# The product of P and V moved ahead of the next item's scores in the slots of the mixing stage

## The reference, cut to what matters

```python
# first model: heads of 64, each query sees a window of keys, with a learned bias
s = jnp.einsum('bhrqd,bhrwkd->bhrqwk', qb, kb).astype(jnp.float32) * scale
s = s + bias[None].astype(jnp.float32)
p = jax.nn.softmax(s.reshape(B, H, rows, COL_BLOCK, wh * COL_SLAB), axis=-1)
outs.append(jnp.einsum('bhrqwk,bhrwkd->bhrqd', p, vb))
# second model: 4 heads of forgetting attention, 4 of dilated attention with rotated q and k
p = jax.nn.softmax(jnp.where(mask, s, NEG_BIG), axis=-1)
return jnp.einsum('bhqk,bhkd->bhqd', p.astype(v.dtype), v)
```

## Time and profile before

| | us |
|---|---|
| median of 3 runs | 2108.96 |
| lowest, highest | 2106.34, 2109.08 |
| the profiled execution | 2110.61 |
| its span, first to last instruction | 2108.8 |
| TensorE busy with matmuls | 2048.7 (97%) |
| VectorE busy | 1310.0 (62%) |
| ScalarE busy | 1058.2 (50%) |
| mean granted clock of TensorE | 0.988 of 2.4 GHz |

### The profile page before, as it was taken

One profiled execution on the slowest core, in us unless ns is written; L12 is line 12 of the kernel. 1 busy time (PEld: TensorE's weight loads), 2 busy tenths in 40 slices (PEclk: granted clock), 3 DMA queues, 4 the chain that ended last, 5 costly groups with the idle time before them and its releaser, 6 DMA issues.

```text
span 2108.8 us, 26738 instructions
## 1 busy us (share of the span) xinstructions
PE 2048.7 (97%) x11144; PEld 1714.2 (81%) x11144; DVE 1310.0 (62%) x1532; ACT 1058.2 (50%) x1278; POOL 56.6 (3%) x72
## 2 busy tenths in 40 slices
PE   7999999999999999999999999999999999999998
PEld 5888877888888887788788888878888889887886
DVE  5655866555655686655565568765556556976554
ACT  4444565444544556544454456654454445565443
POOL 3200004000000000000000000000000000000000
PEclk9999999999999999999999999999999999999999
DMA  8654336555555433555455543345545554335551
GB/s 279 214 195 162 140 112 178 185 187 192 179 181 194 156 131 110 183 181 195 164 177 182 193 156 136 116 169 191 183 176 198 182 184 175 121 121 182 188 181 59
DMA packets 52217, 357.81 MB, mean 170 GB/s; under 512 B 6592, under 2 KB 7008, under 8 KB 9600
## 3 DMA queue, kind: packets, MB, share of 16 engines
q1 hardware_dynamic: 48960, 350.25, 46.6%
q0 software_dynamic: 2416, 5.51, 1.3%
q10 hardware_dynamic: 720, 0.34, 0.1%
HBM read 355.02 MB, written 1.05 MB: 169 GB/s over the span
## 4 chain that ended last, share of the span: by engine, by line
PE 88%; DVE 6%; ACT 3%; DVEq 1%; issue 1%; DMA 0%; ACTq 0%
PE bank L360 82%; DVE w_lo L1087 2%; PE bank L464 2%; PE bank L520 1%; PE bank L404 1%; ACT w_hi L747 1%; PE bank L601 1%; DVE h_lo L1104 1%; PE bank L566 1%; DMA cos_sin<-positions 0%; PE bank L587 0%; ACT h_hi L767 0%; DVEq L1275 0%; ACTq L920 0%; ACT arena L935 0%
## 5 line engine op out<-in xcount | busy, mean ns | idle before, releaser
L1087 DVE TENSOR_TENSOR w_lo<-raw,w_hi 128x2048 fp32r<-128x2048 f32 x332 | 762.7, 2297 | 387.8 <-ACT w_hi L747 387.4
L747 ACT ACTIVATE w_hi<-raw 128x2048 fp32r<-128x2048 f32 x332 | 634.3, 1911 | 270.9 <-PE bank L360 260.7
L360 PE MATMUL bank<-w_hi,h_hi 128*128 128x512 f32 x1536 | 611.7, 398 | 7.1 <-DVE w_lo L1087 4.1
L360 PE MATMUL bank<-w_hi,h_lo 128*128 128x512 f32 x1536 | 600.4, 391 | 0.0
L360 PE MATMUL bank<-w_lo,h_hi 128*128 128x512 f32 x1536 | 599.7, 390 | 0.0
L360 PEld LDWEIGHTS bank<-w_hi,h_hi 128*128 128x128 f32 x1536 | 289.4, 188 | 71.0 <-DVE w_lo L1087 10.2
L360 PEld LDWEIGHTS bank<-w_hi,h_lo 128*128 128x128 f32 x1536 | 289.0, 188 | 62.1
L360 PE MATMUL bank<-w_hi,act_hi 128*128 128x512 f32 x832 | 330.4, 397 | 6.3 <-DVE act_lo L1384 6.3
L360 PEld LDWEIGHTS bank<-w_lo,h_hi 128*128 128x128 f32 x1536 | 289.8, 189 | 56.5
L360 PE MATMUL bank<-w_lo,act_hi 128*128 128x512 f32 x832 | 326.1, 392 | 0.0
L360 PE MATMUL bank<-w_hi,act_lo 128*128 128x512 f32 x832 | 326.1, 392 | 0.0
(11 more groups left out here) (195 smaller groups left out, 1460.7 us busy)
## 6 DMA issues: line engine op xcount, KB each, us to landing
raw<-stream SPq DMA_DIRECT2D x332, 1024.0 KB, 4.8
arena<-rpb POOLq DMA_DIRECT2D x32, 96.0 KB, 9.3
x<-xt SPq DMA_DIRECT2D x4, 256.0 KB, 7.0
arena<-final_gain POOLq DMA_DIRECT2D x2, 512.0 KB, 4.5
out<-x SPq DMA_DIRECT2D x4, 256.0 KB, 2.8
arena<-c_level POOLq DMA_DIRECT2D x1, 384.0 KB, 3.4
arena<-code_w POOLq DMA_DIRECT2D x2, 128.0 KB, 3.6
arena<-c_att POOLq DMA_DIRECT2D x1, 256.0 KB, 5.0
```

The costliest lines, as they stand in the source:

```text
L360: last = mm(o, a, r, start=start and n == 0, stop=stop and n == len(pairs) - 1)
L747: fn(w_hi[u % SLOTS][:, :], raw[u % RAW][:, :], ACT.Copy).then_inc(hi_done, 1)
L1087: tt(w_lo[u % SLOTS][:, :], raw[u % RAW][:, :], w_hi[u % SLOTS][:, :].bitcast(F32), ALU.subtract).then_inc(lo_done, 1)
```

## The change

In `slot`, the call of `heads` for the item that was transposed at the slot's beginning is moved from behind `scores` (and behind the rotation in slot 9) to a place ahead of both. The transposes and the recurrence's step stay in front of it. No instruction is added or removed, and the lists of the other engines are the same.

```diff
                 if i in SPAN_AFTER[b]:
                     span_step(b, L, SPAN_AFTER[b][i])
+                if turned is not None:
+                    heads(b, L, turned)
                 if item is not None:
                     scores(b, L, item)
                 if b == 1 and i == ROTATE_AFTER:
...
-                if turned is not None:
-                    heads(b, L, turned)
                 if i == RECURRENCE_AFTER[b]:
                     recurrence_out(b, L)
```

## The result

| | before | after |
|---|---|---|
| median (20 runs each) | 2107.30 | 2111.49 |
| lowest, highest | 2103.37, 2112.57 | 2110.04, 2114.07 |
| the profiled execution, its span | 2110.61, 2108.8 | 2110.04, 2108.3 |
| mean granted clock | 0.988 | 0.991 |

The changed kernel is slower by a ratio of 1.0020, with a 95% interval of 1.0013 to 1.0027: 4.2 us, between 2.7 and 5.7. Equal times lie outside the interval; the size is the 0.2% that the prediction took as the least to be told from it. A single pair of executions of this kernel can't be compared by its end, since the runs of one kernel spread over 9 us (before) and 4 us (after).

A forecast was written before the change was run, and what follows sets the result against it. TensorE's own work was taken to bound the kernel (88% of the last-ending chain). Stalls of 1.9 for the first model's two layers plus 2.2 and 2.1 for the second's gave +6.2 us, from 2108.96 to 2115.2; range 2109.5 to 2120.5.

The forecast's parts named there:

- slot 11 of the second model: Largest single term, 0.87: copy ends later because the heads delay the rotation by 0.37, and scores no longer fill the wait.
- Slots 5 to 9 of the first model: Heads wait for the copy that scores had covered: 0.27 in slot 5, 0.13 in 6 to 8, 0.27 in 9.
- slots 14 and 15 of the second: Slot 14: heads already wait for the copy, scores now follow them, 0.55 lost; slot 15: unchanged.
- slot 11 of the first: Scores move into TensorE's 2.55 wait for the mixed result, which ends when it did: 0.
- rival D: Late scores delay the next copy in some 9 more slots by 0.4: +3.6 on top, 2118.8; chance 0.05.
- of the exchanged pieces themselves nothing is gained or lost: Every slot: scores (0.63) and heads (0.59) both still run, so swapping them costs only the stall for the copy.
- Slot 13 of the second model: Copy's end plus 0.05 falls after the scores' old start, so TensorE stalls 0.15.
- Slot 10 of the first model: Long recurrence step covers the copy, and TensorE waits 0.36 for VectorE's copy L1247 anyway: 0.
- rival C: Stalls smaller or partly absorbed, as other engines reach later waits with the delay already paid: +3.1, 2112.1; chance 0.12.
- slot 7 of the second model: Heads stall for the copy after losing the scores as cover: 0.61 in the first layer, 0.54 in the second.
- Rival A: Splitting the first model's slot 11 pause avoids low clock: 2109.6 (both layers) or 2112.4 (one); chance 0.18.
- Rival B: Second model's slot 11 pause grows to about 1.5 and the clock falls: +9 to +11.8, 2118 to 2120.8; chance 0.10.

The follow-up runs named there:

- spare matmuls: Both orders with unread matmuls added in TensorE's pauses: 2098.38 with the old order (ratio 0.9961 to the kernel before), 2104.17 with the new order (0.9988).
- The run with the new order in the covered slots: Old order with unread matmuls in TensorE's pauses, heads moved ahead only in slots 10 (first model), 8 and 12 (second): 2097.71 against 2098.38 without the move.
- the second model alone: Kernel before, with heads moved ahead of the scores in the second model's slots only: 2111.31 against 2107.64, ratio 1.0020.
- the first model alone: Kernel before, with heads moved ahead of the scores in the first model's slots only: 2108.58 against 2107.64, ratio 1.0002.

## Why the prediction held, point by point

**Direction and mechanism: right.** The change costs time because TensorE waits for the copy L935, 0.05 after whose end the heads start. The longer copy shows it in the runs, the earlier transposes in the slots. A second part, also forecast, is the rotation made later by the heads ahead of it, which delays ScalarE up to the copy of slot 11 of the second model; putting that one slot back shows it.

**The size: a third too large.** Forecast +6.2, measured +4.2 (2.7 to 5.7), and 5.2 by the slots. The median, 2111.49, lies in the range; against 2115.2 it is 3.7 lower, of which 1.7 is that the median of before fell from 2108.96 (3 runs) to 2107.30 (20 runs). By its own bound for "within 0.2%", 2113.2, it even lies on the side that had 0.29 and not on the one with 0.68; the ratio, 0.20% (0.13 to 0.27), decides neither. That the range held owes something to its width, some 11 us.

**The terms that held.** Slots 5 to 9 of the first model within 0.02 to 0.03 each; slots 14 and 15 of the second within 0.01; slot 11 of the first, which the clock hides in the profiles before and after, is -0.01 in both layers between the two with spare matmuls. Slot 11 of the second model was 0.87 against 0.98, of which the rotation's share was put at 0.37 and is 0.55. The late scores did not come round through VectorE and ScalarE in the first model (rival D): ScalarE was still idle 1.62 ahead of the copy of slot 6, against 1.71.

**The terms that failed.** The step "of the exchanged pieces themselves nothing is gained or lost". Where no stall hides it, the new order takes 0.15 to 0.16 less in slots 8 and 12 of the second model, and 0.34 less in slot 9. What the rows suggest is a cost of each change of form on TensorE, the form being the rows and columns of the array that a matmul uses. In the second model L520 and L601 work on 128 rows by 64 columns of the array, L566 on 64 by 128, the rotation and L360 on 128 by 128. The list L520, L566, L601, L360 has three changes of form; L520, L601, L566, L360 has two. With the rotation in place of L566 it is three before and one after (L520, L601, then rotation, L360). One change less goes with 0.16, two with 0.34. Slot 8 of the second model, the weight loads, before and then after:

```profile
1317.02 0.30 PEld L566 LDWEIGHTS bank<-arena 64*128 64x128 f32 x4
1317.44 0.42 PEld L601 LDWEIGHTS bank<-arena 128*64 128x64 f32 x8
```

```profile
1313.10 0.37 PEld L520 LDWEIGHTS bank<-arena 128*64 128x64 f32 x9
1313.34 0.47 PEld L601 LDWEIGHTS bank<-arena 128*64 128x64 f32 x8
1313.98 0.30 PEld L566 LDWEIGHTS bank<-arena 64*128 64x128 f32 x4 [0.17 <-issue]
```

After, L601's first load starts while L520's still run (the two rows overlap); where the form changes, to L566, the loads pause for 0.17. The Trainium skill, "TensorE: Matmul & The Clock Gate", section "Step-by-step: what each phase is for", has loads pulled ahead of matmuls in flight where row groups don't conflict or the background buffer is meant. These rows have one load that goes ahead (L601 behind L520, of the same form) and one that does not (L566, of another); the page does not name the form as the condition, and no run here shows whether it is that or the row groups. That a change of form is the cause was read from the rows, not tried by itself. The prediction had weighed this rule only for loads behind a semaphore.

Slot 13 of the second model, 0.15 forecast and 0.32 measured, hangs on slot 12: its copy stands behind ScalarE's own list, so the 0.15 that slot 12 saves is waited for again in slot 13. The run with the new order in the covered slots has this part alone, 0.18.

Slot 10 of the first model is another case: its -0.16 is a part of the stall of slot 9 given back. TensorE waits there for VectorE's copy L1247 as before, and came later to it; this is rival C's mechanism, for 0.16 a layer. In sum, these savings (slots 8, 9 and 12 of the second model, 1.3, and slot 10 of the first, 0.3) take 1.6 off the forecast of 6.2, and slots 11 and 13 of the second model put 0.6 back: 5.2.

The other failed term is slot 7 of the second model, 0.61 and 0.54 forecast. It was 0.28 and 0.93 in the profile after, 0.62 and -0.05 with the second model alone, 0.59 and 1.51 with the spare matmuls. It is no fixed term: as far as the profiles tell, the copy there ends a chain of VectorE and ScalarE that runs on its own, and TensorE's place against it depends on how long it ran at 1.2 GHz before, as the windows from 1274 above show.

**Rival A: its pauses came, its gain is not shown.** It had 0.18. The two pauses of slot 11 of the first model became 1.08 and 1.91 instead of 0.45 and 2.55, as forecast, and in the profile after the clock was low behind them for half as long. But single profiles do not tie this to the order. The window from 310 has a clock of 0.83 in two profiles of the old order (before, and the second model alone), 0.91 in three (the changed kernel, the doubled copy in the old order, the early transposes in the new order), and 1.00 in three more: the first model alone, the doubled copy in the new order, and the early transposes in the old order. The last has pauses of 0.46 and 2.51, nearly those of the kernel before; its window:

```profile
310.00:330.00 20.00, 16.14 (x83) 12.29 (x82) 14.60 (x26) 13.46 (x23) 0.00 (x0) 1.00 0.43 152
```

Over all runs on record the mean granted clock is 0.9902 in the changed kernel (20 runs) and 0.9899 in the kernel before (the 65 runs beside the experiments). In those 65, 0.001 of clock goes with 1.3 us, so an estimate of what the clock gave back is 0.4 us, of the 2.8 or 5.6 that rival A had. Nor does the distance of 5.8 with the spare matmuls, against 4.2 without, show a gift of the clock: 1.3 of the 1.6 between them are the larger stalls of slots 5 and 7, and the intervals allow none at all.

**Rival B** did not happen at 1.57, and happened at 2.23 and 1.97.

**What was said of a single profile.** The forecast was built on one execution 1.65 above the median of three; it was 3.3 above the median of twenty. In that profile the clock fell behind each of the seven pauses of 2.5 us and more in mid-program, for 6.8 us each time; in the profile after, four of the falls there were half as long. The sum of slots is not touched by this, but its translation into a time is.

## What to carry to other kernels

Between a producer's transpose and the consumer's matmul on TensorE, the work in between is cover for a copy on another engine: compare the copy's end with the consumer's place before exchanging them, and price each place by the part that sticks out; where it is covered, count how often the matmuls change form, which seems to be what is left. A delay of work that others wait for (the rotation here) shows up where their chain ends, not where it was made. And where TensorE pauses for about 2 us or more, price the clock with the pause: spare matmuls in the pauses were worth twice what the order of the slots was.

## What was not expected of the hardware

- The clock fell to 1.2 GHz after pauses of 2.23 and 1.97 in the middle of dense work, and behind pauses of 0.45 and 2.55 with 0.6 of matmuls between them, but once not behind 0.46 and 2.51. It did not fall after 1.57. The same lists of the first model (the changed kernel, and the first model alone) gave 0.91 in one profile and 1.00 in the other over the 20 us from 310.
- A good part of the spread between runs of the kernel before goes with these falls: over 65 runs the time rises as the mean granted clock falls, 1.3 us for each 0.001. In experiments of 11 runs each the spread was 5 to 7 us without the spare matmuls, and 2.6 and 4.3 with them.
- Matmuls of float32 whose result nobody reads keep the clock up. In the profile of the old order with them, TensorE still waits 0.59 for the mixed result behind those of slot 11 (2.55 before), so they made nothing later there.
- A change of form between float32 matmuls (128 rows by 64 columns, 64 by 128, 128 by 128) goes with some 0.16 of lost time on TensorE in three slots of each layer of the second model; L601 behind L520, of the same form but other tensors, starts without such a pause.
